# First attention pass of an encoder block: one projection unit in another bank, key transposes spread, conditioning steps moved, outputs emptied a slot earlier

## What is computed

```python
mod = silu(c) @ w_ada + b_ada                       # six vectors of 1024: shift, scale, gate, twice
h = rms_norm(x, norm1_gain) * (1 + sc1) + sh1
cb, cc, cu, q, k, v, ga, gb = split(h @ w_in)       # 4 key/value heads, 16 query heads of 64
y_a = cb * dwconv3(cc * cu, conv_w)
y_b = windowed_gqa(rms_norm(q, q_gain), rms_norm(k, k_gain), v, sink)   # |t-s| <= 128, softmax with a sink
x = x + g1 * ((sigmoid(ga) * y_a + sigmoid(gb) * y_b) @ w_o)
h = rms_norm(x, norm2_gain) * (1 + sc2) + sh2
a, b = split(h @ w_up)
x = x + g2 * ((gelu(dwconv3(a, ffn_conv_w) + ffn_conv_b) * b) @ w_down)
```

## Time and profile before

| what | us |
|---|---|
| median of 3 runs | 806.92 (805.38 to 809.6) |
| the profiled execution | 808.3 |
| its span on the core | 806.2 |
| PE busy | 774.8 (96%) |
| DVE busy | 515.6 (64%) |
| ACT busy | 374.2 (46%) |
| POOL busy | 374.2 (46%) |

### The profile page before, as it was taken

One profiled execution on the slowest core, in us unless ns is written; L12 is line 12 of the kernel. 1 busy time (PEld: TensorE's weight loads), 2 busy tenths in 40 slices (PEclk: granted clock), 3 DMA queues, 4 the chain that ended last, 5 costly groups with the idle time before them and its releaser, 6 DMA issues.

```text
span 806.2 us, 10380 instructions
## 1 busy us (share of the span) xinstructions
PE 774.8 (96%) x3709; PEld 644.4 (80%) x3709; DVE 515.6 (64%) x722; ACT 374.2 (46%) x664; POOL 374.2 (46%) x223
## 2 busy tenths in 40 slices
PE   3889999999999999999999999999999999999997
PEld 3677787788888888878889988888888888888886
DVE  5847876658765976686638799888888988000000
ACT  7665467455654575556524454434443343112220
POOL 2774423343453345244863255554444555444340
PEclk9999999999999999999999999999999999999999
DMA  8943342243414341533143042223333322323311
GB/s 301 381 146 116 134 155 78 72 164 131 158 54 181 131 157 52 184 130 108 57 150 105 4 154 85 75 100 104 104 104 104 98 75 76 104 92 118 131 52 40
DMA packets 83279, 96.03 MB, mean 119 GB/s; under 512 B 2674, under 2 KB 77610, under 8 KB 83242
## 3 DMA queue, kind: packets, MB, share of 16 engines
q1 hardware_dynamic: 79018, 93.44, 34.0%
q10 hardware_dynamic: 4224, 2.10, 0.8%
HBM read 93.43 MB, written 2.10 MB: 118 GB/s over the span
## 4 chain that ended last, share of the span: by engine, by line
PE 85%; DVE 9%; ACT 3%; issue 2%; DMA 1%; SPq 0%; DVEq 0%
PE bank L832 25%; PE bank L833 25%; PE bank L834 25%; PE bank L964 2%; PE bank L992 2%; PE bank L975 2%; DVE acc L1283 1%; DVE bank L1195 1%; DVE pt_lo L1347 1%; DMA ada<-in_w_ada_dram 1%; DVE a_buf L1371 1%; DVE sm L1333 1%; DVE prob L1326 1%; PE bank L881 1%; PE bank L880 1%
## 5 line engine op out<-in xcount | busy, mean ns | idle before, releaser
L832 PE MATMUL bank<-h_hi,w_hi 128*128 128x512 f32 (+1 forms) x760 | 294.8, 388 | 2.3 <-DVE q_st L1245 2.3
L833 PE MATMUL bank<-h_lo,w_hi 128*128 128x512 f32 (+1 forms) x760 | 292.4, 385 | 0.0
L834 PE MATMUL bank<-h_hi,w_lo 128*128 128x512 f32 (+1 forms) x760 | 292.2, 384 | 0.0
L450 POOL TENSOR_TENSOR w_lo<-w_raw,w_hi 128x1024 fp32r<-128x1024 f32 x76 | 194.8, 2585 | 195.4 <-ACT w_hi L546 188.1
L457 POOL TENSOR_TENSOR w_lo<-w_raw,w_hi 128x512 fp32r<-128x512 f32 x88 | 123.8, 1428 | 181.1 <-ACT w_hi L546 181.1
L546 ACT ACTIVATE w_hi<-w_raw 128x1024 fp32r<-128x1024 f32 x120 | 122.5, 1052 | 100.4 <-PE bank L834 100.4
L832 PEld LDWEIGHTS bank<-h_hi,w_hi 128*128 128x128 f32 x760 | 143.4, 189 | 30.0 <-issue 2.7
L834 PEld LDWEIGHTS bank<-h_hi,w_lo 128*128 128x128 f32 x760 | 143.6, 189 | 28.7
L833 PEld LDWEIGHTS bank<-h_lo,w_hi 128*128 128x128 f32 x760 | 143.7, 189 | 26.5
L832 PE MATMUL bank<-g_hi,w_hi 128*128 128x512 f32 x176 | 69.2, 393 | 0.0
L834 PE MATMUL bank<-g_hi,w_lo 128*128 128x512 f32 x176 | 68.6, 390 | 0.0
(11 more groups left out here) (186 smaller groups left out, 1056.9 us busy)
## 6 DMA issues: line engine op xcount, KB each, us to landing
w_raw<-in_w_in_dram SPq DMA_DIRECT2D x23, 1024.0 KB, 5.1
w_raw<-in_w_up_dram SPq DMA_DIRECT2D x21, 1024.0 KB, 4.9
ada<-in_w_ada_dram SPq DMA_DIRECT2D x32, 512.0 KB, 6.0
ada<-in_w_ada_dram SPq DMA_DIRECT2D x32, 256.0 KB, 6.3
w_raw<-in_w_down_dram SPq DMA_DIRECT2D x8, 1024.0 KB, 4.7
w_raw<-in_w_o_dram SPq DMA_DIRECT2D x4, 1024.0 KB, 4.9
w_raw<-in_w_down_dram SPq DMA_DIRECT2D x4, 768.0 KB, 4.2
x_nat<-in_x_dram SPq DMA_DIRECT2D x4, 512.0 KB, 5.2
```

The lines of the kernel that those rows point to most:

```text
L450: pool.tensor_tensor(lo_of(n, u), raw(n)[:, :, u * P:(u + 1) * P], hi_of(n, u), SUB).then_inc(lo_ready, 1)
L832: pe.matmul(dst, w_h, rhs_hi, start=first, stop=False)
L833: pe.matmul(dst, w_h, rhs_lo, start=False, stop=False)
L834: return pe.matmul(dst, w_l, rhs_hi, start=False, stop=last)
```

## The change

- The unit (C, u = 0) of pass 0 goes to bank 6 instead of bank 0 (`unit_bank`). Bank 0 is next needed by (U, u = 0) in S4, and the waits for its drain move there. ACT copies the unit out before it copies the values (`v_st`), no longer at slot 2. Key 0 is turned in the same bank 6 and now waits for that copy.
- In the last step `t` = 7 of the start, PE's query row with the low part of h stands between the second and the third block of keys and values, not after the fourth: four matmuls earlier.
- `K_TURN` is `{4: (0,), 6: (1,), 7: (2,), 8: (3,)}`; `k_n` lies in `merged` instead of `prob`.
- `query_sums(0, 1)` moves to slot 4, `query_norm(0)` and ACT's root to slot 5.
- In pass 0 the steps 1 to 7 of `gemv` stand four slots later (step n at slot 2n + 8, step 0 at slot 4 as before).
- POOL makes the low part of the unit pair U in halves and begins at `kn_half`, not at `kn_ready`.
- `heads_low` and `heads_out` are done in `pv_slot` itself, in all passes.
- The eleven transfers of parameters are issued by POOL, before its first tile of the start, not by SP. PE turns them after the fourth group of x, and ACT copies them before the groups 4 to 7. ACT's first weight step (`start_high(0)`) comes after those groups. `hT[0..2]` lie in a buffer of their own, so that POOL makes them without waiting for all eight groups.

```diff
-        k_n = spare[:, NB * PC:3 * NB * PC].rearrange("p (b j o d) -> p b j o d", b=NB, j=KV, o=2)
+        k_n = merged[:, KT - NB:KT, :].rearrange("p b (j o d) -> p b j o d", j=KV, o=2)
+        hT = [n_first[:, t, :] if t < 3 else x_rows[:, t, :] for t in range(KT)]
+        def unit_bank(n, u):
+            return bank[OB if (n, u) == (P_MIX + 1, 0) else u][:, :]
-        K_TURN = {3: (0,), 4: (1, 2), 5: (3,)}
+        K_TURN = {4: (0,), 6: (1,), 7: (2,), 8: (3,)}
+        Q0_NORM = 5
-        GEMV_AT = {n + 1: n for n in range(KT)}
+        GEMV_AT = [{n + 1 + (2 if n else 0): n for n in range(KT)}] + [{n + 1: n for n in range(KT)}] * (KV - 1)
...
-            parameters()                      # SP
+            parameters()                      # POOL, the same transfers
             pool.wait_ge(r_copy, 1)
-            pool.wait_ge(xt_done, KT)
             for t in range(KT):
+                if t == 3:
+                    pool.wait_ge(xt_done, KT)
...
-            pool.wait_ge(kn_ready, 1)
-            low(None, 0, P_MIX + 2)
+            pool.wait_ge(kn_half, 1)
+            for u in range(2):
+                low_by_halves(P_MIX + 2, u)
...
+            unit(pair_of(0, 0), 0)
+            act.wait_ge(mix_free, 1)
+            act.activation(a_buf[:, 0, :], unit_bank(pair_of(0, 0), 0), ACT.Copy).then_inc(g_act, 1)
             for b in range(NB):
                 act.wait_ge(kn_ready, b + 1)
                 act.activation(v_st[:, b, :, 0, :], v_heads(b), ACT.Copy).then_inc(v_high, 1)
-            root(None, 0, 2, NB * HG, 1, 2)
+                    if g == 0 and slot == Q0_NORM:
+                        root(None, 0, 2, NB * HG, 1, 2)
...
-                        if slot == pv_slot(g, b) + 1:
+                        if slot == pv_slot(g, b):
                             heads_low(b)
...
+                    if b == 2 and last:
+                        query_low_row()
...
                 if j == 0:
                     pe.wait_ge(kn_ready, NB)
+                    pe.wait_ge(g_act, act_drains(0, "C", 0))
...
-                    if kind == "C" and not g or kind == "G" and g < KV - 1:
+                    if not g and (kind, u) in (("C", 1), ("U", 0)) or kind == "G" and g < KV - 1:
...
+                    if g == 0 and slot == Q0_NORM - 1:
+                        query_sums(0, 1)
+                    if g == 0 and slot == Q0_NORM:
+                        query_norm(0)
...
-                        if slot == pv_slot(g, b) + 1:
+                        if slot == pv_slot(g, b):
                             heads_out(b)
```

72 lines of the change are left out of this document (37 added, 35 removed).

## The result

The changed kernel is slower, by 0.7%: 813.27 us in the median of 5 runs (810.77 to 814.49) against 807.35 (5 runs, 805.38 to 809.6), a ratio of 1.0066 with a 95% interval of 1.0038 to 1.0093. Forecast were 797.5 and "faster". Its profiled execution took 810.77 (span 808.6); that of before took 808.3 (span 806.2). The forecast for this execution was 798.9, so 11.9 us are to be explained.

The account below looks back on a forecast made before the run. PE's summed work bounds the kernel (busy 774.8 of 806.2 us). Ceiling 12.3 us (8.48 waits, 3.4 clock, 0.4 first matmuls) less 1.0, 0.5, 1.1 and 0.3 gave 9.4 us: 797.5 against median 806.92, range 794.0 to 802.5.

Parts of the forecast that it names:

- Outputs emptied in `pv_slot`: Value products of pass 0: 1.72 us wait goes, 1.1 stays in place of 0.99; later passes nothing.
- a new wait of over 1 us in passes 1 to 3: Sign listed under what would show the prediction wrong: PE waiting anew in the later passes.
- Unit in bank 6, query row earlier: S0 of pass 0: PE starts the unit at 57.5; the whole 2.32 us wait and its clock are won.
- Keys spread: Key turns at S4, S6, S7, S8: the 1.45 us wait for a `key_low` goes.
- First scores: DVE's first scores, behind step 0's tile: 1.0 us charged for a new PE wait in S6, between 0 and 2.2.
- Conditioning steps later: Scores of block 1, pass 0: the 2.00 us wait and its clock go; 0.5 us kept for blocks by POOL.
- Parameters by POOL: Start: 0.3 us of loss taken, between 0 and 4.9 us, by what a transfer costs POOL to issue.
- C: Rival: parameters come late at 1.28 us per transfer, start loses 4.9 us in place of 0.3: 802.1; chance 0.10.
- D: Rival: slower than before, PE's start queues behind the parameters; at 2.4 us per transfer 813; chance 0.04.
- A: Rival: DVE bounds S6 to S10, a wait reaches 2 us and the clock falls: 801.0; chance 0.20 together with E.
- B: Rival: no new wait, tile lands early and POOL blocks nothing: 794.6 to 795.6; chance 0.10.
- E: Rival: PE leaves S0 on time but is held at S2 or S4 by query or key: 800; chance 0.20 with A.

Follow-up runs that it names:

- the held GpSimd: Changed kernel, with POOL in each pass waiting for both merges before its sixth pair of low steps: 804.95 us, 0.9958 of before.
- late emptying: Changed kernel with `heads_low` and `heads_out` back one slot after `pv_slot`: 803.69 us, 0.9936 of before.
- the old start: Changed kernel with the start of before (parameters issued by SP, turned after all groups of x): 811.98 us, 1.0048 of before.
- early emptying for blocks 1 and 2: Changed kernel, outputs emptied early only for blocks 1 and 2 of pass 0: 806.06 us, 0.9973 of before; with the start of before, 805.51 us, 0.9965.

## Why the prediction was wrong

**The step that failed** is "Outputs emptied in `pv_slot`". It counted what the emptying gains and what it costs the next value product, and put the rest at nothing: for the first pass it names the emptying "ahead of the weight copy" in ACT's slot 20 and goes on only to the wait of 1.1; for the later passes it ends with "so DVE does not wait there. Nothing." It asked whether DVE or PE would wait for ACT, and not what stands *behind* the emptying on ACT: the weight copies that release POOL. The first of them came 3.0 us later against PE's schedule and put POOL's low steps onto DVE's merges.

The price can be read from PE's times at the same work in both kernels. The lead of the changed kernel is 6.57 us at the start of pass 1 and 2.8 behind the second pair of scores there; 2.8 and 2.0 around the same place of pass 2; 1.85 and 1.0 around that of pass 3. It is -0.2 at the value product of pass 3, -1.8 behind the fall of the clock there, and -2.5 from 402 us to the end. So 3.8, 0.8 and 0.9 us fall at the three pairs of scores (a wait, and a slower first matmul behind it), 1.2 at the value product and 1.6 in the clock: 8.3 of the 11.9 us. The first three are shown by the held GpSimd, the 1.2 only by its rows and its going with late emptying. The rows needed were in the trace of before: a merge step of 1.35 beside 0.69 where POOL ran, and I had read the 2.42 of the earlier trace rows as just such a block, yet priced blocks only in S6 to S10. None of the rivals had this mechanism. The place was named only among the signs that would prove it wrong ("a new wait of over 1 us in passes 1 to 3").

**The rest of the 11.9** lies mostly before pass 1. The unit starts at 59.62 where 57.5 and the 0.3 charged for the parameters make 57.8: 1.8 us. The transposes of x took 3.39 us for 16 at 16.44 where the earlier trace rows has 1.91, and the first product came 0.95 later than before. From it to the unit PE took 36.45 us, against 35.24 to 35.27 in five executions with full clock and 35.92 in a sixth; so the low clock from 23.5 to 26.9 cost up to 1.2 there. As the old start had the same or worse in both of its profiles, and the same mean, the new order is not the cause; what sets these times is open. The wait for the first scores adds 0.6; 0.7 came better than forecast in S10 and S22; 0.3 is a new wait at the head of pass 1. Some 1.6 us I can't assign, 0.8 of them before pass 1.

Point by point:

- *Unit in bank 6, query row earlier*: right in result. PE goes from the last key products (from 59.17) to the unit (59.62) without a gap, and the clock is 1.00. The unit came at 57.18 to 57.65 in five of the six later profiles with full clock from the first product on, where I had 57.5. The earlier row alone was worth the 0.9 forecast; of the other 1.42 some 0.6 reaches the end in the profile.
- *Keys spread*: the sign was wrong. With the keys in their old slots the 1.45 us are gone too, even with the unit in bank 0, and the spreading added 1.3 us of wait at the first scores. I had credited the 1.45 to the spreading and not asked which other part removes it.
- *First scores*: mechanism right, the tile lands late (DVE waits 3.46 us for it, until 77.92, then the four small steps and the scores at 79.50). Charged 1.0, measured 1.64, and 1.36 to 1.60 in the other kernels with spread keys. SP issued the tile at 71.92, not at 69.3; 2.0 of that is the late start (69.88 with late emptying, where the unit starts at 57.58).

```profile
71.92 1.05 SPq L401 DMA_DIRECT2D ada<-in_w_ada_dram  x2
77.92 0.75 DVE L1298 TENSOR_SCALAR acc<-ada,c_act 128x1024 f32<-128x1024 f32 x1 [3.46 <-DMA ada<-in_w_ada_dram]
```

- *Conditioning steps later*: the wait at S10 and its clock are gone, and I had kept 0.5 for it that didn't come. But with the other parts in place they were worth some 1 us (a wait of 1.12 and no fall of the clock), not the 2.00 and 1.7 counted. And the step that now stands in slot 22, priced at nothing, is ahead of the merges.
- *Outputs in pass 0*: the 1.72 gone, 0.85 left of the 0.99, where I had 1.1.
- *Parameters by POOL*: the 0.3 holds. PE doesn't wait for them at 16.27, so the ten have landed by then, and one transfer costs POOL some 0.5 us to issue, near the short end of my bounds:

```profile
5.35 1.05 POOL L476 DMA_DIRECT2D w_raw<-in_norm_gain_dram  x2
9.87 0.57 POOL L486 DMA_DIRECT2D sink_b<-in_sink_dram  x1
```

The landing by 16.27 speaks against the estimate of 24.3 us from the Trainium skill ("DMA: Bandwidth & Descriptors", on the anatomy of one DMA), and the trap of its page "SBUF — State Buffer" did not spring with DVE idle. C and D fell; that the kernel is slower than before, as D has it, is not by D's mechanism. A fell as well (no wait at S10), B too, and of E's two places S2 and S4 neither held PE.

## What to carry to other kernels

An instruction that is moved ahead of others on an in-order engine delays or hastens everything behind it. For each of those, look at whom it releases, and what the released engine will run beside. Price two engines that work on SBUF at the same time from the trace's own pairs (here 0.69 alone, 1.7 together), not from each alone. And when several parts remove the same wait, price each with the others in place: here the spread of the keys was counted as a gain of 1.45 us, and undoing it won some 1.5.

## What the runs showed of the hardware

The collision is mutual and near to taking turns, but not quite: behind the first (2.26), POOL's low steps took some 1.7 us each, while DVE made a merge step beside each, where 0.69 and 1.26 alone make 1.95. From 146.24 to the end of the last merge near 154.1 are 7.85 us; in them the two engines did 7.8 us of low steps and merges and the last 1.1 us of a conditioning step. Running them together won some 1 us out of 8.9.

The fall of the clock isn't settled by the length of the wait ahead of it. The same wait of 2.25 us at the same place was followed by 1.2 GHz for a while in the kernel with early emptying for blocks 1 and 2 and the old start, and by 1.00 throughout with the new start; the wait of 3.35 in the changed kernel was followed by 1.00, that of 2.80 by 0.57 over 4 us. By the windows each fall took 1.7 us of work, and four of them 3.4 (behind the 2.77 at 348.22 in the kernel with GpSimd held, and at the start of three others). At the start, waits of 2.43, 2.66 and 2.79 were followed by full clock, and waits of 2.62 and 2.72 by half. A sum that counts a fall as certain, or as gone, is off by such a step in single executions; the medians of the kernels with fewer long waits are what carries.
